# The halo's gated product computed with channels on partitions and its 32 tokens as moving operand, then turned back by four transposes

## The chip, the cores and the metric

The kernel runs on all 8 cores of one Trainium2 chip. Each core works alone on its own 2048 of the 16384 positions, plus a halo of 32 positions ahead of them; nothing is exchanged between cores. The metric is device time in microseconds of the slowest core, over the whole program.

## What is computed

One decoder layer: a mixing sub-layer, a cross-attention into 256 memory tokens, and a SwiGLU feed-forward net, each between two RMS norms with a residual. The change touches the convolution branch (group B) of the mixing:

```python
def parallel_conv_mixer(h, w_mix_in, conv_a_w, conv_b_w, conv_b_b, ln_b_g, ln_b_b, w_mix_out):
    u = jnp.einsum("bsd,dc->bsc", h, w_mix_in)      # 2560 columns
    b_a, c_a, v_a, glu_v, glu_g = jnp.split(u, [D_A, 2 * D_A, 3 * D_A, 3 * D_A + D_B], axis=-1)
    y_a = b_a * causal_dwconv(c_a * v_a, conv_a_w)
    z = glu_v * jax.nn.sigmoid(glu_g)               # 512 channels
    z = causal_dwconv(z, conv_b_w) + conv_b_b       # 31 taps, causal
    y_b = jax.nn.silu(layernorm(z, ln_b_g, ln_b_b))
    y = jnp.concatenate([y_a, y_b], axis=-1)
    return jnp.einsum("bsc,cd->bsd", y, w_mix_out)
```

A convolution with 31 taps needs z of the 30 positions ahead of a core's own ones. Those come from the halo: 32 tokens whose gated product z each core computes for itself, once.

## The kernel before

A core handles its 2048 positions in two tiles of 1024 (`mid(0, ...)`, `mid(1, ...)`), each tile being 8 blocks of 128 tokens. There is no planner: every engine (PE, ACT, DVE, POOL, SP) runs its instructions in the order in which the Python code is written, and waits by semaphores that a small scheduler derives from the buffers' keys. So the order of the calls is the order in each engine's queue.

PSUM is used in two ways. `pair()` hands out three double banks in turn (pp1, pp2, pp3) for matmul results; `tbank()` hands out the two halves of pp0 in turn, for transposes.

The part around the change, in order, for the first tile:

- `glu(7)`: value and gate columns of the last block, 16 matmuls of 512 columns. `glu_ev` evicts: ACT takes tanh of the gate half, DVE multiplies (`stt`) into `zst`. (The gate's sigmoid is made from tanh; the factor 0.5 is in the convolution's weights.)
- `build_wc(0..7)`: eight DVE products of 128x2560 that spread the convolution's taps into `wconv`. Parts 1 and 2 stand behind `glu_ev(7)`, part 3 behind the halo's expansion, parts 4 to 7 in the hooks of `cv_unit`.
- `halo_z` (L552): `hh` holds the 32 halo tokens, transposed. It is the stationary operand (128x32), and `wing`, the weights, moves: 16 matmuls of 512 columns. The result has tokens on 32 partitions and channels in the free dimension. ACT and DVE evict it to `zh` (32x512).
- `halo_expand` (L557): DVE spreads `zh` into `zhe` (32x4096) with a mask, after a small cast to `selT`.
- `mid(0)` (L691): `cv_unit(0, 0)` computes C*v of the first 128 channels: two halves (h = 0, 1) of 16 matmuls, each followed by an ACT copy and a DVE product, then the hook (`build_wc(4 + h)`); then for t = 0 another 16 matmuls of 32 columns with `winc` stationary and `hh` moving, with an ACT copy and a DVE product to `cvh`. Then `halo_zp` (L562): 32 small matmuls that gather `zhe` to the convolution's layout, and a DVE cast into `zp`. Then `z_t` (L571): four groups q of 8 transposes of `zst`, through the two halves of pp0 in turn; q = 0 and 2 are copied out by ACT, q = 1 and 3 by DVE. Then `cv_unit(0, 1)` in the same manner, with `build_wc(6 + h)`, and then the convolution's 160 matmuls (`conv`), which need `zp`, the halo's part of it too.

In the profile matmuls and transposes all bear the lines of the helpers: L374 is `mm`, L433 is `tr`, L354 `act`, L357 `tt`, L367 `stt`, L371 `cp`.

Of the kernel before, what the change touches and what calls it, by code (L numbers as in the profile page):

```python
# [7 lines left out]
BF16 = mybir.dt.bfloat16  # L8
# [5 lines left out]
D = 1024  # L14
# [186 lines left out]
def build_program():  # L201
# [26 lines left out]
    with ExitStack() as stack:  # L228
# [34 lines left out]
        def gbuf(shape, dt, off, keys, group):  # L263
            t = sbt(shape, dt, off)
            nbytes = int(np.prod(shape[1:])) * (4 if dt == F32 else 2)
            for k in keys:
                S.place(k, off, off + nbytes, group)
            return t
# [104 lines left out]
        def mm(out, lhsT, rhs, start, stop, reads, writes, signal):  # L373
            S.op("pe", lambda e: e.matmul(out, lhsT=lhsT, rhs=rhs, start=start, stop=stop), reads, writes, signal)  # L374
# [116 lines left out]
        def evslot():  # L491
            evc[0] += 1
            return evc[0] % 3
# [7 lines left out]
        def glu_mms(lhs, lk, pt, bk, n=128):  # L501
            for h in range(2):
                for kc in range(8):
                    mm(pt[0:n, h * 512:(h + 1) * 512], lhs(kc), wing[:, 2 * h:2 * h + 2, kc, :], kc == 0, kc == 7,
                       [lk, "wg%d" % (4 * h + kc // 4), "wg%d" % (4 * h + 2 + kc // 4)], [bk[h]], kc == 7)

        def glu_evict(pt, bk, groups, nu, n=128):
            s = evslot()
            pv = pt[0:n, 0:nu * 256].rearrange("p (u k c) -> p u k c", k=2, c=128)
            act(ev[0:n, s, 0:nu * 128].rearrange("p (u c) -> p u c", c=128), pv[:, :, 0, :], AF.Tanh,  # L510
                bk[0:(nu + 1) // 2], ["ev%d" % s], scale=0.5)

            def second():
                for u0, u1, out, okey in groups:
                    stt(out.rearrange("p (u g) c -> p u g c", g=8),
                        ev[0:n, s, u0 * 128:u1 * 128].rearrange("p (u g c) -> p u g c", g=8, c=GC), 1.0,
                        pv[:, u0:u1, 1, :].rearrange("p u (g c) -> p u g c", c=GC), ADD, MUL,
                        ["ev%d" % s] + bk[0:(nu + 1) // 2], [okey])
            return second
# [25 lines left out]
        def build_wc(part):  # L545
            gd = NG * ND // 8
            a = part * gd
            tt("dve", wconv[:, a:a + gd, :].rearrange("p a (c r) -> p a c r", r=P),
               wsb[:, a * P:(a + gd) * P].rearrange("p (a r) -> p a r", r=P).unsqueeze(2).broadcast_to([128, gd, GC, P]),
               mkb[:, :, :].unsqueeze(1).broadcast_to([128, gd, GC, P]), MUL, ["mkb", "wsb"], ["wc%d" % part])  # L550

        def halo_z():  # L552
            pt, bk = pair()
            glu_mms(lambda kc: hh[:, kc, :], "hh", pt, bk, HALO)
            return glu_evict(pt, bk, [(0, 4, zh[:, :, :], "zh")], 4, HALO)

        def halo_expand():  # L557
            cp("dve", selT[:, 0:HT], sm[0:HALO, SM_SEL:SM_SEL + HT], ["sm"], ["selT"])
# [3 lines left out]
        def halo_zp():  # L562
            pt, bk = pair()
            for g in range(NG):
                mm(pt[:, g * HT:(g + 1) * HT], zhe[:, g, :, :].rearrange("p s c -> p (s c)"), selT[:, 0:HT], True, True,
                   ["zhe", "selT"], [bk[0]], g == NG - 1)
            cp("dve", zp[:, :, 0:HT], pt[:, 0:NG * HT].rearrange("p (g t) -> p g t", t=HT), [bk[0]], ["zph"])
# [62 lines left out]
        def cv_unit(t, c, after=None):  # L630
            for h in range(2):
                pt, bk = pair()
                hk = ["h%d" % b for b in range(4 * h, 4 * h + 4)]
                for n in range(2):
                    for kc in range(8):
                        mm(pt[:, n * 512:(n + 1) * 512], winc[:, c, kc, n * 128:(n + 1) * 128],
                           hT[:, kc, h * 512:(h + 1) * 512], kc == 0, kc == 7, ["wcv%d" % c] + hk, [bk[n]], kc == 7)
                s = evslot()
                act(ev[:, s, :], pt[:, 0:512], AF.Copy, [bk[0]], ["ev%d" % s])
                tt("dve", cvx[:, c, (2 + 4 * h) * TAU:(6 + 4 * h) * TAU], pt[:, 512:1024], ev[:, s, :], MUL,  # L640
                   ["ev%d" % s, bk[1]], ["cv%d" % c])
                if after is not None:
                    after(h)
            if t == 0:
                pt, bk = pair()
                for n in range(2):
                    for kc in range(8):
                        mm(pt[:, n * 512:n * 512 + HALO], winc[:, c, kc, n * 128:(n + 1) * 128], hh[:, kc, :],
                           kc == 0, kc == 7, ["wcv%d" % c, "hh"], [bk[n]], kc == 7)
                s = evslot()  # L650
                act(ev[:, s, 0:HALO], pt[:, 0:HALO], AF.Copy, [bk[0]], ["ev%d" % s])
                tt("dve", cvh[:, c, :], pt[:, 512:512 + HALO], ev[:, s, 0:HALO], MUL, ["ev%d" % s, bk[1]], ["cvh%d" % c])
                cp("pool", car[:, c, :], cvh[:, c, :].rearrange("p (s t) -> p s t", s=P)[:, 6:8, HT - 1],
                   ["cvh%d" % c], ["car%d" % c])
            v = cvx[:, c, :].rearrange("p (s t) -> p s t", t=TAU)
            cp("pool", v[:, 0:2, 0], car[:, c, :], ["car%d" % c], ["cv%d" % c])
            cp("pool", v[:, 0:2, 1:TAU], v[:, P:P + 2, 0:TAU - 1], ["cv%d" % c], ["cv%d" % c])
            cp("pool", car[:, c, :], v[:, P:P + 2, TAU - 1], ["cv%d" % c], ["car%d" % c])
# [32 lines left out]
        def mid(t, after_conv, fill, fill_t):  # L691
            cv_unit(t, 0, (lambda h: build_wc(4 + h)) if t == 0 else None)
            if t == 0:
                halo_zp()
            z_t(t)
            cv_unit(t, 1, (lambda h: build_wc(6 + h)) if t == 0 else None)
            conv_a(0)
            conv(t)
            fill()
            after_conv()  # L700
            conv_a(1)
            cv_unit(t, 2, lambda h: ln_stats(0, 4) if h == 0 else None)
            ln_rstd(0, 4)
            b_unit(0)
            ln_bias(0, 4)
            ln_stats(4, 8)
            ln_norm(0, 4)
            ln_rstd(4, 8)
            b_unit(1)
            ln_bias(4, 8)  # L710
            conv_a(2)
            fill_t()
            cv_unit(t, 3, lambda h: ln_norm(4, 8) if h == 0 else None)
            conv_a(3)
            b_unit(2)
            n_t(0, 2)
            b_unit(3)
            n_t(2, 4)

        hh = gbuf([128, 8, HALO], BF16, C0 + 4 * D * 4 + 2048, ["hh"], None)  # L720

        def wload_c(c):
            wload("wcv%d" % c, winc[:, c], winc_d[:, c], ["wcv%d" % c])
# [66 lines left out]
        glu_ev(7, *g)  # L790
        build_wc(1)
        build_wc(2)
        halo_z()()
        halo_expand()
        build_wc(3)

        def load_s(s, src, reads=()):
# [463 lines left out]
```

How the kernel before makes its waits and increments, by code:

```python
            def body(e):  # L184
                for (waits, fn, inc) in lists[engname]:
                    for (sk, v) in waits:
                        e.wait_ge(sems[sk], v)
                    if fn is not None:
                        ins = fn(e)
                        if inc is not None:
                            ins.then_inc(sems[inc[0]], inc[1])
```

## Time and profile before

| | us |
|---|---|
| median of 3 runs | 889.1 (887.85 to 889.79) |
| the profiled execution, all cores | 889.61 |
| its spans, core by core | 884.3 to 887.0 |
| core 7, the slowest: span | 887.0 |
| mean granted TensorE clock of the cores | 0.996 to 0.999 |

A span runs from a core's first to its last instruction; the time of an execution also holds what lies around the spans. All rows below are of core 7. In the page's table (core 4, 886.4 us) PE is busy for 849.1 us (96% of the span), DVE for 390.0, ACT for 298.3, POOL for 125.9; the chain that ended last is PE for 92%. The stretch of the change lies between 55 and 85 us, in the fourth and fifth of the 40 slices.

In rows on matmuls, `128*32` is the stationary operand (rows x columns) and `128x512` the moving one. A matmul's duration in a row is from its start to the end of its way through the array; the next one starts long before that end. `LDWEIGHTS` on PEld is the load of the stationary operand, which overlaps PE. "idle" and the name behind "<-" say how long the engine had nothing to do before, and who released it.

### The profile page before, as it was taken

How to read it: one execution, taken by the hardware profiler on the slowest of the kernel's cores; microseconds unless marked ns; L12 is line 12 of the kernel's file. 1: busy time of each engine (PE TensorE's matmuls, PEld its weight loads, DVE VectorE, ACT ScalarE, POOL GpSimd, SP SyncE). 2: the span in 40 equal slices, each digit the busy share in tenths (PEclk: the TensorE clock that was granted, in tenths of full speed). 3: DMA queues.
4: the chain of work that ended last, by engine and by line, in shares of the span. 5: the costliest groups of instructions: out<-in, count | busy, mean ns of one | idle time of the engine just before them, and what ended most of it. 6: DMA issues, size and time to landing. Idle time of an engine off the chain costs nothing.

```text
span 886.4 us, 13126 instructions; the slowest of 8 cores (884.3 to 887.0 us)
## 1 busy us (share of the span) xinstructions
PE 849.1 (96%) x4795; PEld 432.8 (49%) x4872; DVE 390.0 (44%) x500; ACT 298.3 (34%) x544; POOL 125.9 (14%) x290
## 2 busy tenths in 40 slices
PE   2899999999999899999999999999999999999997
PEld 1657444555664455554444444444444444444443
DVE  1477758437547678886522122331232322221122
ACT  2332345532636668765331111221122211111111
POOL 3121113112103132321110010000000000000000
PEclk9999999999999999999999999999999999999999
DMA  9599057368894257877696012122121121210011
GB/s 195 153 179 192 1 185 253 124 128 139 168 221 91 50 148 188 190 153 184 194 182 118 1 72 95 37 60 72 72 95 36 48 84 72 67 53 1 1 48 71
DMA packets 33327, 97.94 MB, mean 110 GB/s; under 512 B 11344, under 2 KB 11472, under 8 KB 32368
## 3 DMA queue, kind: packets, MB, share of 16 engines
q0 software_dynamic: 7344, 33.03, 23.4%
q1 hardware_dynamic: 25920, 64.07, 21.5%
q8 instruction: 39, 0.64, 0.3%
q14 instruction: 24, 0.20, 0.1%
HBM read 107.05 MB, written 20.97 MB: 144 GB/s over the span
## 4 chain that ended last, share of the span: by engine, by line
PE 92%; ACT 3%; issue 2%; DMA 1%; DVE 1%; DVEq 0%; SPq 0%; POOL 0%; POOLq 0%; ACTq 0%
PE pp L374 89%; PE pp L433 3%; ACT t L354 3%; DMA t<-x 1%; DVE t L1003 1%; DVE t L367 0%; ACT L354 0%; DVEq L1193 0%; SPq L377 0%; DVE t L371 0%; POOLq L1193 0%; ACT pp L354 0%; POOL t L357 0%; ACTq L187 0%; POOL t L363 0%
## 5 line engine op out<-in xcount | busy, mean ns | idle before, releaser
L374 PE MATMUL pp<-t,t 128*128 128x512 bf16 (+2 forms) x4195 | 819.2, 354 | 7.9 <-ACT t L354 2.7
L374 PEld LDWEIGHTS pp<-t,t 128*128 128x128 bf16 x4272 | 397.0, 98 | 411.2 <-issue 6.9
L357 DVE TENSOR_TENSOR t<-pp,t 128x512 bf16<-128x512 f32 (+4 forms) x173 | 150.4, 873 | 365.8 <-PE pp L374 194.7
L354 ACT ACTIVATE t<-pp 128x512 f32<-128x512 f32 (+5 forms) x208 | 153.3, 750 | 355.8 <-PE pp L374 336.6
L367 DVE SCALAR_TENSOR_TENSOR t<-t,t,t 128x1024 bf16<-128x1024 f32 (+4 forms) x100 | 126.5, 1271 | 49.3 <-POOL t L357 29.7
L361 POOL TENSOR_SCALAR t<-t 128x1 f32<-128x1 f32 (+2 forms) x102 | 24.7, 242 | 627.5 <-ACT t L354 323.3
L433 PE MATMUL pp<-t,t 128*128 128x128 bf16 (+1 forms) x600 | 43.2, 222 | 23.0 <-DVE t L367 19.8
L354 ACT ACTIVATE pp<-pp 128x1024 f32<-128x1024 f32 (+1 forms) x17 | 16.3, 958 | 142.4 <-PE pp L374 142.4
L357 POOL TENSOR_TENSOR t<-t,t 128x1 f32<-128x1 f32 (+2 forms) x103 | 60.7, 589 | 15.6 <-POOL t L361 0.6
L354 ACT ACTIVATE t<-pp,t 128x256 bf16<-128x256 f32 (+2 forms) x76 | 43.9, 583 | 42.8 <-DVE t L1003 34.2
L354 ACT ACTIVATE t<-t 128x1024 bf16<-128x1024 f32 (+2 forms) x52 | 53.9, 1037 | 8.7 <-DMA t<-x 8.7
L433 PEld LDWEIGHTS pp<-t,t 128*128 128x128 bf16 (+1 forms) x600 | 37.8, 99 | 35.4 <-issue 26.8
L361 DVE TENSOR_SCALAR t<-t,t 128x256 bf16<-128x256 bf16 (+1 forms) x80 | 30.3, 378 | 7.2 <-DVE t L361 0.5
L354 ACT ACTIVATE t<-t,t 128x512 bf16<-128x512 bf16 (+1 forms) x24 | 20.7, 916 | 26.7 <-DVE t L367 16.6
L1003 DVE TENSOR_REDUCE t<-pp 128x4 f32<-128x1024 f32 x16 | 19.5, 1220 | 6.9 <-PE pp L374 6.8
L371 POOL COPY t<-t 128x2 bf16<-128x2 bf16 (+2 forms) x29 | 11.2, 388 | 78.3 <-DVE t L357 72.1
L367 DVE SCALAR_TENSOR_TENSOR t<-t,pp 128x128 bf16<-128x128 f32 (+3 forms) x29 | 12.5, 461 | 22.0 <-ACT t L354 21.4
L371 DVE COPY t<-pp 128x1024 bf16<-128x1024 bf16 x25 | 17.1, 683 | 6.2 <-PE pp L433 6.1
L357 DVE TENSOR_TENSOR t<-t,t 128x2560 bf16<-128x2560 bf16 (+1 forms) x9 | 14.0, 1570 | 0.0
L377 POOL DMA_DIRECT2D t<-w_gu x22 | 13.6, 618 | 0.3 <-issue 0.3
L354 ACT ACTIVATION_READ_ACCUMULATOR t<-pp,t 128x1 f32 x64 | 12.3, 193 | 0.0
L361 DVE TENSOR_SCALAR t<-pp,t 128x1024 bf16<-128x1024 f32 x4 | 5.1, 1284 | 15.1 <-PE pp L374 15.1
(26 smaller groups left out, 65.2 us busy)
## 6 DMA issues: line engine op xcount, KB each, us to landing
t<-x SPq DMA_DIRECT2D x68, 512.0 KB, 6.7
x<-t SPq DMA_DIRECT2D x24, 512.0 KB, 3.6
t<-w_gu POOLq DMA_DIRECT2D x22, 512.0 KB, 6.8
out<-t SPq DMA_DIRECT2D x15, 512.0 KB, 2.8
t<-w_dn POOLq DMA_DIRECT2D x6, 768.0 KB, 20.2
t<-gains SPq DMA_DIRECT2D x6, 512.0 KB, 9.4
t<-w_ing POOLq DMA_DIRECT2D x8, 256.0 KB, 16.5
t<-w_inc POOLq DMA_DIRECT2D x4, 512.0 KB, 10.4
```

Source lines behind the costliest of these rows:

```text
L354: S.op("act", lambda e: e.activation(out=out, in_=in_, func=func, **kw), reads, writes)
L357: S.op(eng, lambda e: e.tensor_tensor(out=out, in0=in0, in1=in1, op=op), reads, writes)
L361: S.op(eng, lambda e: e.tensor_scalar(out=out, in0=in0, scalar1=s1, scalar2=None, op0=op0), reads, writes)
L367: S.op("dve", lambda e: e.scalar_tensor_tensor(out=out, in0=in0, scalar=sc, in1=in1, op0=op0, op1=op1), reads, writes)
L371: S.op(eng, lambda e: e.tensor_copy(out=out, in_=in_), reads, writes)
L374: S.op("pe", lambda e: e.matmul(out, lhsT=lhsT, rhs=rhs, start=start, stop=stop), reads, writes, signal)
L377: return S.dma(eng, sem, lambda e: e.dma_start(out=out, in_=in_), reads, writes)
L433: S.op("pe", lambda e: e.transpose(out, in_, ident[0:n, 0:n]), reads + ["ident"], writes, signal)
L1003: S.op("dve", lambda e: e.tensor_reduce(out=mx[:, m, 0:4], in_=pt[:, :].rearrange("p (h n) -> p h n", h=4), axis=AX.X, op=ALU.max, negate= ...
```

## The change

`halo_z` swaps the operands. For each of 4 chunks of 128 channels, for gate and value (k = 0, 1), and for each of 8 slices of the contraction, the weights of 128x128 are stationary and `hh` moves with its 32 tokens: 64 matmuls of 32 columns in place of 16 of 512. The results lie in 256 columns of one PSUM bank, channels on partitions. ACT's tanh and DVE's product now work on 128x128 elements in place of 32x512 and write `zhT`, a new buffer in a free part of the region that holds `hh`.

A new function `halo_t` turns `zhT` back: four transposes into a half of pp0 (`tbank()`), and a DVE copy of 32x512 from there to `zh`. It stands between `cv_unit(0, 0)` and `z_t(0)`, where `halo_zp` stood. `halo_expand` moves from its place behind `halo_z` to behind `z_t(0)`, and `halo_zp` into the hook of `cv_unit(0, 1)` behind its first half, ahead of `build_wc(6)`.

```diff
--- before.py
+++ after.py
@@ -551,8 +551,23 @@
 
         def halo_z():
             pt, bk = pair()
-            glu_mms(lambda kc: hh[:, kc, :], "hh", pt, bk, HALO)
-            return glu_evict(pt, bk, [(0, 4, zh[:, :, :], "zh")], 4, HALO)
+            for c in range(4):
+                for k in range(2):
+                    for kc in range(8):
+                        mm(pt[:, (2 * c + k) * HALO:(2 * c + k + 1) * HALO], wing[:, c, kc, k * 128:(k + 1) * 128],
+                           hh[:, kc, :], kc == 0, kc == 7, ["hh", "wg%d" % (2 * c + kc // 4)], [bk[0]],
+                           c == 3 and k == 1 and kc == 7)
+            s = evslot()
+            pv = pt[:, 0:8 * HALO].rearrange("p (c k n) -> p c k n", k=2, n=HALO)
+            tv = ev[:, s, 0:4 * HALO].rearrange("p (c n) -> p c n", n=HALO)
+            act(tv, pv[:, :, 0, :], AF.Tanh, [bk[0]], ["ev%d" % s], scale=0.5)
+            stt(zhT[:, :, :], tv, 1.0, pv[:, :, 1, :], ADD, MUL, ["ev%d" % s, bk[0]], ["zhT"])
+
+        def halo_t():
+            pv, bk = tbank()
+            for c in range(4):
+                tr(pv[0:HALO, c * 128:(c + 1) * 128], zhT[:, c, :], 128, ["zhT"], [bk], c == 3)
+            cp("dve", zh[:, :, :].rearrange("p g c -> p (g c)"), pv[0:HALO, 0:512], [bk], ["zh"])
 
         def halo_expand():
             cp("dve", selT[:, 0:HT], sm[0:HALO, SM_SEL:SM_SEL + HT], ["sm"], ["selT"])
@@ -691,9 +706,17 @@
         def mid(t, after_conv, fill, fill_t):
             cv_unit(t, 0, (lambda h: build_wc(4 + h)) if t == 0 else None)
             if t == 0:
-                halo_zp()
+                halo_t()
             z_t(t)
-            cv_unit(t, 1, (lambda h: build_wc(6 + h)) if t == 0 else None)
+            if t == 0:
+                halo_expand()
+
+            def hook(h):
+                if h == 0:
+                    halo_zp()
+                build_wc(6 + h)
+
+            cv_unit(t, 1, hook if t == 0 else None)
             conv_a(0)
             conv(t)
             fill()
@@ -718,6 +741,8 @@
             n_t(2, 4)
 
         hh = gbuf([128, 8, HALO], BF16, C0 + 4 * D * 4 + 2048, ["hh"], None)
+
+        zhT = gbuf([128, 4, HALO], BF16, C0 + 4 * D * 4 + 2560, ["zhT"], None)
 
         def wload_c(c):
             wload("wcv%d" % c, winc[:, c], winc_d[:, c], ["wcv%d" % c])
@@ -790,8 +815,7 @@
         glu_ev(7, *g)
         build_wc(1)
         build_wc(2)
-        halo_z()()
-        halo_expand()
+        halo_z()
         build_wc(3)
 
         def load_s(s, src, reads=()):
```

On PE, from the halo tokens' own transposes to the last products of `cv_unit(0, 1)` (t1_43 is `wing`, t39_81 the transposed tokens `hT`, t72_114 `hh`, t2_44 `winc`, t26_68 `selT`, t12_54 `zst`, t73_115 `zhT`, t69_111 the unit matrix; the order of before with - and of now with +):

```order
 L374 MATMUL pp3<-t1_43,t39_81 128x512 x16
-L374 MATMUL pp1<-t1_43,t72_114 32x512 x16
+L374 MATMUL pp1<-t72_114,t1_43 128x32 x64
 L374 MATMUL pp2<-t39_81,t2_44 128x512 x16
 L374 MATMUL pp3<-t39_81,t2_44 128x512 x16
 L374 MATMUL pp1<-t72_114,t2_44 128x32 x16
-L374 MATMUL pp2<-t26_68,t21_63 128x4 x32
+L433 MATMUL pp0<-t69_111,t73_115 32x128 x4
 L433 MATMUL pp0<-t69_111,t12_54 128x128 x32
-L374 MATMUL pp3<-t39_81,t2_44 128x512 x16
+L374 MATMUL pp2<-t39_81,t2_44 128x512 x16
+L374 MATMUL pp3<-t26_68,t21_63 128x4 x32
```

The halo's matmuls become 64 short ones at the same place, four transposes through pp0 come ahead of the 32 of `z_t`, and the 32 gathering matmuls (128x4) move from ahead of `z_t` to behind the first 16 of `cv_unit(0, 1)`.

On DVE, from the product of `glu(7)` (t12_54) to the cast into `zp` (t14_56), before (t4_46 is `wconv`, t22_64 `zh`, t21_63 `zhe`, t41_83 the C*v products, t24_66 `cvh`, t14_56 `zp`, t26_68 `selT`):

```order
L367 SCALAR_TENSOR_TENSOR t12_54<-t50_92,pp3 128x32x16
L357 TENSOR_TENSOR t4_46<-t42_84,t43_85 128x2560 x2
L367 SCALAR_TENSOR_TENSOR t22_64<-t50_92,pp1 32x512
L371 CAST t26_68<-t65_107 32x4
L357 TENSOR_TENSOR t21_63<-t22_64,t44_86 32x4096
L357 TENSOR_TENSOR t4_46<-t42_84,t43_85 128x2560
L357 TENSOR_TENSOR t41_83<-pp2,t50_92 128x512
L357 TENSOR_TENSOR t4_46<-t42_84,t43_85 128x2560
L357 TENSOR_TENSOR t41_83<-pp3,t50_92 128x512
L357 TENSOR_TENSOR t4_46<-t42_84,t43_85 128x2560
L357 TENSOR_TENSOR t24_66<-pp1,t50_92 128x32
L371 CAST t14_56<-pp2 128x32x4
```

and now, from the two `wconv` products behind that product of `glu(7)` to the expansion (t73_115 is `zhT`):

```order
L357 TENSOR_TENSOR t4_46<-t42_84,t43_85 128x2560 x2
L367 SCALAR_TENSOR_TENSOR t73_115<-t50_92,pp1 128x128
L357 TENSOR_TENSOR t4_46<-t42_84,t43_85 128x2560
L357 TENSOR_TENSOR t41_83<-pp2,t50_92 128x512
L357 TENSOR_TENSOR t4_46<-t42_84,t43_85 128x2560
L357 TENSOR_TENSOR t41_83<-pp3,t50_92 128x512
L357 TENSOR_TENSOR t4_46<-t42_84,t43_85 128x2560
L357 TENSOR_TENSOR t24_66<-pp1,t50_92 128x32
L371 COPY t22_64<-pp0 32x512
L371 COPY t14_56<-pp0 128x8x128 x2
L371 CAST t26_68<-t65_107 32x4
L357 TENSOR_TENSOR t21_63<-t22_64,t44_86 32x4096
```

The copy of 32x512 into t22_64 is new; it stands behind the fifth `wconv` product of this list and the `cvh` product, and ahead of the copies of `z_t`. The expansion of 32x4096 moves from ahead of the third `wconv` product to behind the copies of `z_t`.

## Rows read from the trace of the kernel before

**Rows 1.** Stretches of core 7: PE busy (instructions), granted clock, DMA share, GB/s.
```profile
20.00:30.00 10.00, 7.58 (x41) 1.00 0.98 259
...
55.00:95.00 40.00, 39.18 (x386) 1.00 0.82 171
```

**Rows 2.** Chain that ended last, core 7, 51 to 92 us: start us, us, what.
```profile
51.65 3.45 PE pp L374 x16
...
55.39 15.40 PE pp L374 x112
70.80 0.57 PE pp L433 x8
...
71.45 1.03 ACT t L354
72.48 0.14 issue
```

**Rows 3.** PE timeline, core 7: start, us, instruction, xcount [idle before <-releaser].
```profile
70.73 1.07 PE L433 MATMUL pp<-t,t 128*128 128x128 bf16 x16
72.61 1.05 PE L433 MATMUL pp<-t,t 128*128 128x128 bf16 x16 [0.82 <-ACT t L354]
73.50 10.71 PE L374 MATMUL pp<-t,t 128*128 128x512 bf16 x106
...
25.88 1.01 PE L433 MATMUL pp<-t,t 128*128 128x128 bf16 x8 [2.42 <-DVE t L367]
```

**Rows 4.** PE and PEld groups by form, 55 to 95 us: xcount | busy, mean ns | idle.
```profile
L374 PE MATMUL pp<-t,t 128*128 128x128 bf16 x160 | 9.1, 219 | 0.0
...
L374 PE MATMUL pp<-t,t 128*128 128x32 bf16 x32 | 1.1, 176 | 0.0
L374 PE MATMUL pp<-t,t 32*128 32x4 bf16 x32 | 0.9, 159 | 0.0
...
L374 PEld LDWEIGHTS pp<-t,t 128*128 128x128 bf16 x298 | 20.0, 98 | 12.5 <-issue 0.4
```

**Rows 5.** The same view in 5 ns of the first 16-matmul burst, 69.700 to 69.705 us.
```profile
L374 PE MATMUL pp<-t,t 128*128 128x32 bf16 x7 | 0.3, 176 | 0.0
```

**Rows 6.** DVE timeline, core 7, columns as in rows 3.
```profile
63.30 0.68 DVE L367 SCALAR_TENSOR_TENSOR t<-t,pp 32x512 bf16<-32x512 f32 x1
63.90 0.15 DVE L371 CAST t<-t 32x4 bf16<-32x4 f32 x1
64.08 3.68 DVE L357 TENSOR_TENSOR t<-t,t 32x4096 bf16<-32x4096 bf16 x2
...
69.70 0.69 DVE L357 TENSOR_TENSOR t<-pp,t 128x512 bf16<-128x512 f32 x1
70.31 1.48 DVE L357 TENSOR_TENSOR t<-t,t 128x2560 bf16<-128x2560 bf16 x1
71.71 0.18 DVE L357 TENSOR_TENSOR t<-pp,t 128x32 bf16<-128x32 f32 x1
71.81 0.28 DVE L371 CAST t<-pp 128x128 bf16<-128x128 f32 x1
...
73.77 0.69 DVE L371 COPY t<-pp 128x1024 bf16<-128x1024 bf16 x1 [1.09 <-PE pp L433]
77.23 0.69 DVE L357 TENSOR_TENSOR t<-pp,t 128x512 bf16<-128x512 f32 x1 [2.76 <-PE pp L374]
```

**Rows 7.** DVE groups by form, 20 to 180 us: xcount | busy, mean ns | idle.
```profile
L357 DVE TENSOR_TENSOR t<-pp,t 128x1024 f32<-128x1024 f32 x8 | 9.8, 1222 | 6.5 <-ACT t L354 6.5
...
L357 DVE TENSOR_TENSOR t<-pp,t 128x512 bf16<-128x512 f32 x8 | 5.5, 686 | 4.7 <-PE pp L374 4.2 <-ACT t L354 0.5
L371 DVE COPY t<-pp 128x1024 bf16<-128x1024 bf16 x5 | 3.4, 687 | 3.6 <-PE pp L433 3.6
L367 DVE SCALAR_TENSOR_TENSOR t<-t,pp 128x128 bf16<-128x128 f32 x12 | 2.8, 282 | 10.4 <-ACT t L354 10.4
...
L357 DVE TENSOR_TENSOR t<-t,t 32x4096 bf16<-32x4096 bf16 x1 | 2.3, 2279 | 0.0
```

## The prediction

> **What bounds the kernel now.** I read the stretches first. Between 55 and 95 us, which holds everything that the change touches, PE is busy for 39.18 of 40.00 us at a granted clock of 1.00 [rows 1]: the full one of TensorE's two levels, 2.4 GHz. The chain that ended last [rows 2] says the same in order of time: PE alone from 55.39 us for 15.40 us, then eight transposes, then ACT's copy of the first group of `z_t` (1.03 us), then PE again. So whatever shortens PE's work here counts, as long as PE does not then wait for somebody. The only wait in the stretch is 0.82 us in the middle of `z_t` [rows 3]: the third group of transposes needs the half of pp0 from which ACT is still copying the first. Then I read DVE's timeline [rows 6], since the change puts one more DVE instruction between two steps of PE. From 63.30 us on DVE goes from one instruction to the next without idle time until the copies of `z_t`. Its queue is full of `wconv` products of 1.4 us each that nobody needs yet, and whatever stands behind them has to wait.
>
> **The halo's matmuls.** Before: 16 matmuls of 512 columns. Sixteen such take 3.45 us (216 ns each) [rows 2]. Now: 64 of 32 columns, each with its own 128x128 weights. The trace has that very form, in the bursts of 16 that `cv_unit` runs for the halo. Its duration is 176 ns and 7 are under way at any instant [rows 5], so one starts every 25 ns. Two such bursts keep PE busy for 1.1 us, or 34 ns each with the way through the array counted twice; the 32 matmuls of 4 columns take 0.9 us, or 28 ns each [rows 4]. I take 27 ns: 64 x 27 = 1.73 us, so 1.72 us less on PE. The ends are 25 (1.60 us) and 34 (2.18 us); the trace has bursts of 16 directly followed by 32, not of 64, so a higher end stands among the rivals.
>
> The Trainium skill ("TensorE: Matmul & The Clock Gate", section "Wait — 56ns, not 53.3ns?") gives a floor of about 25 ns from start to start of small matmuls, which the trace bears out with 25; it also says that with hardware decode off the sequencer spends about 62 ns on each matmul. By that the halo would take 64 x 62 = 3.97 us, 2.24 more than my term, and the kernel 891.4; the 28 ns of the gathering matmuls here speak against it.
>
> **The eviction.** ACT's tanh and DVE's product shrink: 676 ns or so of DVE (0.68, [rows 6]) against 282 ns for a 128x128 product [rows 7]. Nobody waits for either. The product stands behind `wconv` products until 63.2 us, and `zhT` is wanted only some 5 us later. This part is worth nothing in itself.
>
> **The transposes back.** Four transposes with 128 moving columns. The convolution's 160 of that width take 9.1 us [rows 4], so 57 ns each: 0.23 us more on PE. I allow nothing else for them, since `zhT` is long there.
>
> **The new copy, and who stands behind it.** `halo_t` takes one half of pp0. The first group of `z_t` gets the other, and the second group gets the half of `halo_t` again, so it has to wait until DVE has copied `zh` out of it. That copy stands in DVE's queue behind the C*v product of the second half of `cv_unit(0, 0)`, the `wconv` product from its hook and the small `cvh` product. I follow it in the clock of core 7:
>
> - Before, `z_t` starts at 70.73 [rows 3]. Going back by the gathering matmuls (0.90) and by 16 of 32 columns (0.45), the second half of `cv_unit(0, 0)` ended at 69.38. Now it ends 1.72 earlier, at 67.66.
> - PE: 16 small matmuls to 68.11, four transposes to 68.34, first group of `z_t` (8 x 56 ns) to 68.79. Then it waits.
> - DVE: a product starts 0.28 us after PE's last matmul (73.50 + 16 x 0.216 = 76.95 against 77.23, [rows 3, 6]), so at 67.94. From it to the `wconv` product 0.61, from there to `cvh` 1.40, to the next 0.10 [rows 6]: the copy starts at 70.05.
> - The copy: 1222 ns for 1024 and 686 for 512 elements of a product give 150 ns fixed; a copy of 1024 bf16 takes 687 [rows 7], so 0.52 ns an element, and 512 take 0.42 us. Bounds are 0.28 (the 128-element cast) and 0.69. It ends at 70.47, and a PE that waited starts 0.14 later [rows 2]: 70.61. **PE waits 1.82 us.**
> - Second and third group to 71.50; ACT has copied the first by about 70.1, so the old wait of 0.82 goes. The fourth needs the half of the second: DVE's copy starts 0.27 after that group (73.50 against 73.77, [rows 3, 6]), at 71.32, takes 0.69, and with 0.14 PE goes on at 72.15. A new wait of 0.65. `z_t` ends at 72.60.
>
> Before, it ended at 73.50 [rows 3]: 0.90 earlier now. But the gathering matmuls, 0.90 us, no longer lie in front of it; they come behind the next 16 matmuls. Sum so far: 0.00.
>
> **The moved expansion.** It was hidden and far ahead; now it has to be ready when the first half of `cv_unit(0, 1)` ends at 72.60 + 3.45 = 76.05. DVE: last copy of `z_t` at 72.87, next at 73.48, cast 0.18 (63.90 to 64.08), expansion 2.28 [rows 6, 7]: it ends at 75.94, with 0.14 at 76.08. A tie, with 0.03 us of waiting. The cover is PE's 16 matmuls, and there is nothing to spare: each tenth that DVE comes later is paid. The gathering then takes the 0.90 already counted. Behind it stand the cast into `zp`, `wconv` parts 6 and 7, and the product of the second half. PE's second half gives DVE 3.45 us for 0.28 + 1.4 of work, so the queue is caught up, and the convolution finds the engines as before. POOL and SP get nothing new.
>
> **The sum.** Halo matmuls -1.72, transposes back +0.23. Waits in `z_t`, all from start to start: +1.82 + 0.65 for the new ones, and for the old one 72.61 less 71.63 (70.73 + 16 x 56 ns), 0.98; the 0.82 of its row counts from the end of the last transpose's way through the array. Together +1.49. Wait for the expansion +0.03. The sum is +0.03 us. The profiled execution took 889.61 us and would take 889.6; that is 0.5 above the median of the runs, 889.1, so I forecast **889.1**. By the bounds: 25 ns gives -0.13, 34 ns +0.45, the copy at 0.28 or 0.69 gives -0.14 or +0.27.
>
> **Rivals.**
>
> *The gain comes through.* If DVE served the copy at once (say the `wconv` product were not between, which the order excludes), PE would wait only for ACT as before: -1.72 + 0.23 = -1.5 us, with 25 ns -1.6. That gives 887.5 to 887.6. Against it speaks DVE's queue, which is in order in every row; for it only that PE's early start might let DVE's queue slip differently than I draw it.
>
> *Short matmuls do not keep their pace.* In a burst of 64 the instructions or the weights' loads may not come fast enough. The loads take 98 ns each when alone [rows 4] and overlap only because many are under way; a pair of load and matmul of 128 columns takes 57 ns. At 57 ns the halo takes 3.65 us, 1.92 above my 1.73. PE then still waits the same 1.8 us, because DVE's copy is released by PE, and the kernel ends at 891.1 (with the 0.03 of the sum); wholly exposed, at 98 ns, 6.27 in place of 1.73, 893.7. It decides from 55 ns on, where the loss is 28 ns x 64 = 1.8 us.  Against it: 48 short matmuls in a row already run at 25 to 28 ns while the DMA engines are just as busy.
>
> *The expansion comes late.* If DVE is later by half a microsecond (a copy that waits longer, a slower product beside DMA traffic), PE waits for `zhe` behind 16 matmuls: +0.5, 889.6. Likely enough, but too small to be told from nothing.
>
> *The clock falls* in the new wait of 1.8 us. PE idled 2.42 us at 25.9 us, and the granted clock there and around it reads 1.00 [rows 1, 3]. I give it no chance of its own.
>
> **How the numbers follow.** A measurement here tells about 0.2% (1.8 us) from no change; the largest gain that the rows allow, 1.6 us, is under that. Chances: the wait eats the gain, with or without a late expansion, 0.84 (all of it within 0.2%); the gain comes through 0.07 (887.5: at the edge, and half of it would read as same); short matmuls slow 0.07 (mostly over 0.2%); something small elsewhere 0.02. The three runs shown spread from 887.85 to 889.79, so about 0.03 on each side goes to readings that stray past 0.2%. Together: faster 0.07, same 0.84, slower 0.09. The range goes from the gain that comes through (887.5) to slow matmuls at 57 ns (891.1), which leaves out 1 to 2 in 10.
>
> **What would show it.** In the profile of the changed kernel: a group of 64 matmuls 128x32, some 1.7 us long, ahead of `cv_unit(0, 0)`; ACT's and DVE's halo instructions at 128x128; in `z_t` of the first tile a PE idle of about 1.8 us released by DVE's copy (L371) after the first eight transposes, one of 0.65 by DVE's copy before the last eight, and none by ACT; the first 512-column matmuls of `cv_unit(0, 1)` some 0.9 us earlier than at 73.50 on a core with the same start; little or no idle before the 128x4 matmuls. I am wrong if the idle in `z_t` is much shorter (then it is faster), if the 64 take over 3 us, or if PE waits for `zhe` by a microsecond or more.

## The result, and the profile of the changed kernel

| | before | changed |
|---|---|---|
| median of 20 runs, us | 888.45 | 890.54 |
| ratio to before on the same chip | | 1.0014 (1.0008 to 1.0021) |
| profiled execution, us | 889.61 | 889.46 |
| its spans, core by core, us | 884.3 to 887.0 | 883.4 to 887.9 |
| mean granted clock of its cores | 0.996 to 0.999 | 0.993 to 0.999 |

By the ratio, which sets runs against runs of before on the same chip and is the measure here (the medians lie 2.1 us apart), the changed kernel is slower by 0.14%, about 1.2 us, where no change at all was forecast. One run of the kernel before (1004.9 us) and two of the changed one (about 1060 us), in which one die ran at a lower clock, are left out of the ratio. The 0.14% are less than the 0.2% that I called the limit of what can be told, but 19 runs against 18 tell it: the interval does not reach 1. So something costs a microsecond or more that is not in my sum.

Around the change nearly everything is as forecast. The chain of the slowest core, core 5 (start us, us, what), now goes from PE to DVE and back, twice, where in [rows 2] it went once over ACT:

```profile
53.53 12.46 PE pp L374 x128
...
66.38 1.58 DVE t L357 x2
67.97 0.33 DVE t L371
68.30 0.14 issue
...
69.14 0.70 DVE t L371
...
69.98 0.76 PE pp L433 x8
```

PE's timeline of the same core shows the two waits, both released by DVE's copies (L371), 1.56 and 0.50 us of idle in place of the 0.82 for ACT in [rows 3]:

```profile
65.92 0.95 PE L433 MATMUL pp<-t,t 128*32 128x128 bf16 x12
68.43 1.05 PE L433 MATMUL pp<-t,t 128*128 128x128 bf16 x16 [1.56 <-DVE t L371]
69.98 0.76 PE L433 MATMUL pp<-t,t 128*128 128x128 bf16 x8 [0.50 <-DVE t L371]
70.53 5.62 PE L374 MATMUL pp<-t,t 128*128 128x512 bf16 x30
```

DVE's timeline is the queue that I drew, to a few hundredths (compare [rows 6]): the product of the second half of `cv_unit(0, 0)`, `wconv` part 5, the `cvh` product, then the copy of `zh` in 0.40 us (0.42 in the forecast).

```profile
65.78 0.69 DVE L357 TENSOR_TENSOR t<-pp,t 128x512 bf16<-128x512 f32 x1 [0.80 <-PE pp L374]
66.38 1.48 DVE L357 TENSOR_TENSOR t<-t,t 128x2560 bf16<-128x2560 bf16 x1
67.78 0.18 DVE L357 TENSOR_TENSOR t<-pp,t 128x32 bf16<-128x32 f32 x1
67.88 0.40 DVE L371 COPY t<-pp 32x512 bf16<-32x512 bf16 x1
69.14 0.69 DVE L371 COPY t<-pp 128x1024 bf16<-128x1024 bf16 x1 [0.86 <-PE pp L433]
...
71.52 2.27 DVE L357 TENSOR_TENSOR t<-t,t 32x4096 bf16<-32x4096 bf16 x1
75.83 0.69 DVE L357 TENSOR_TENSOR t<-pp,t 128x512 bf16<-128x512 f32 x1 [2.04 <-PE pp L374]
```

The expansion (71.52 us) is done at 73.79. And the groups by form, 55 to 95 us: 96 matmuls of 32 columns (64 of the halo, 32 of `cv_unit`) and four transposes of `zhT`:

```profile
L374 PE MATMUL pp<-t,t 128*128 128x32 bf16 x96 | 2.9, 176 | 0.0
...
L433 PE MATMUL pp<-t,t 128*32 128x128 bf16 x4 | 0.4, 222 | 0.0
```

Two rows above do not fit the sum, though. The last eight transposes take 0.55 us to the start of the next matmuls (69.98 to 70.53) where eight take 0.45. And DVE's product of the first half of `cv_unit(0, 1)` starts at 75.83, while 16 matmuls from 70.53 with DVE's 0.28 would end at 74.27: it comes 1.56 us late. The stretches of core 5 say why (PE busy with its instructions, granted clock, DMA share, GB/s):

```profile
66.00:70.00 4.00, 1.94 (x29) 1.00 1.02 210
70.00:71.00 1.00, 1.00 (x10) 0.65 0.99 213
71.00:73.00 2.00, 2.00 (x6) 0.50 1.09 223
73.00:74.00 1.00, 1.00 (x4) 0.65 1.08 205
74.00:80.00 6.00, 6.00 (x56) 1.00 1.03 212
```

The granted clock falls to 0.50, the lower of the two levels (1.2 GHz), in the 71st microsecond, and is back at full in the 74th. At half speed 0.70 us in the first of these rows, 2.0 in the second and 0.70 in the third cost 0.35 + 1.0 + 0.35 = 1.7 us. Six of the eight cores show this. Core 1 does not:

```profile
70.00:71.00 1.00, 0.50 (x10) 1.00 1.09 195
71.00:73.00 2.00, 2.00 (x16) 1.00 1.10 222
```

```profile
69.38 1.05 PE L433 MATMUL pp<-t,t 128*128 128x128 bf16 x16 [1.56 <-DVE t L371]
70.93 0.61 PE L433 MATMUL pp<-t,t 128*128 128x128 bf16 x8 [0.50 <-DVE t L371]
71.37 4.82 PE L374 MATMUL pp<-t,t 128*128 128x512 bf16 x49
```

It has the same two waits and the same order, and its last eight transposes take 0.44 us to the next matmuls.

For the whole stretch I take two marks on PE that both kernels have: the start of the eight transposes of the halo tokens (32x32), ahead of `glu(7)`, and the start of the first transposes of `n_t`, behind the convolution and most of the tile's work. Before, on core 7, 59.69 us lie between them (all eight cores: 59.68 or 59.69):

```profile
55.03 0.36 PE L433 MATMUL pp<-t,t 32*128 32x32 bf16 x8
...
114.72 1.06 PE L433 MATMUL pp<-t,t 128*128 128x128 bf16 x16
```

Changed kernel, core 1, without the fall of the clock, 59.53:

```profile
54.12 0.36 PE L433 MATMUL pp<-t,t 32*128 32x32 bf16 x8
...
113.65 1.06 PE L433 MATMUL pp<-t,t 128*128 128x128 bf16 x16
```

Changed kernel, core 5, with it, 61.14:

```profile
53.17 0.36 PE L433 MATMUL pp<-t,t 32*128 32x32 bf16 x8
...
114.31 1.06 PE L433 MATMUL pp<-t,t 128*128 128x128 bf16 x16
```

So the change as such is worth -0.16 to -0.23 us here (cores 1 and 2), and each of the six cores whose clock falls ends up 1.3 to 1.5 us behind the kernel before; the fall itself costs 1.5 to 1.7 us.

The kernel before has such a fall too, at another place, and in both kernels alike. PE waits 2.42 us at about 25 us there, on every core. Its core 5, timeline and stretch:

```profile
24.82 0.61 PE L433 MATMUL pp<-t,t 128*128 128x128 bf16 x8 [2.42 <-DVE t L367]
```

```profile
25.00:30.00 5.00, 5.00 (x37) 0.66 0.93 242
```

Cores 0 to 3, 5 and 6 show this; cores 4 and 7 are dealt with below, where the prediction is answered. 0.34 of 5.00 us are 1.7 us lost, the price of one fall.

### The profile page after: what moved, and what is told of

The parts are those of the page before. It is cut to its first block, busy times and chain, and to the rows that moved or that the text cites. A ratio compares the mean times of both kernels' runs of the same rounds, so it can differ in the third digit from the quotient of the medians.

```text
span 887.9 us, 13309 instructions; the slowest of 8 cores (883.4 to 887.9 us)
## 1 busy us (share of the span) xinstructions
PE 854.0 (96%) x4924; PEld 433.5 (49%) x4924; DVE 390.0 (44%) x501; ACT 298.1 (34%) x544; POOL 125.1 (14%) x290
## 4 chain that ended last, share of the span: by engine, by line
PE 92%; ACT 3%; DVE 1%; DMA 1%; issue 1%; DVEq 0%; SPq 0%; POOL 0%; POOLq 0%; ACTq 0%
PE pp L374 89%; PE pp L433 3%; ACT t L354 3%; DMA t<-x 1%; DVE t L1027 1%; DVE t L367 0%; DVE t L357 0%; DVE t L371 0%; ACT L354 0%; DVEq L1217 0%; SPq L377 0%; POOLq L1217 0%; ACT pp L354 0%; POOL t L357 0%; ACTq L187 0%
## 5 line engine op out<-in xcount | busy, mean ns | idle before, releaser
L374 PE MATMUL pp<-t,t 128*128 128x512 bf16 (+3 forms) x4320 | 825.5, 352 | 3.8 <-ACT t L354 2.7
L354 ACT ACTIVATE t<-t,t 128x512 bf16<-128x512 bf16 (+1 forms) x24 | 20.7, 916 | 25.6 <-DVE t L367 16.6
L371 POOL COPY t<-t 128x2 bf16<-128x2 bf16 (+2 forms) x29 | 11.0, 380 | 79.8 <-DVE t L357 73.6
L367 DVE SCALAR_TENSOR_TENSOR t<-t,pp 128x128 bf16<-128x128 f32 (+2 forms) x29 | 12.1, 448 | 21.3 <-ACT t L354 20.8
L371 DVE COPY t<-pp 128x1024 bf16<-128x1024 bf16 (+1 forms) x26 | 17.5, 672 | 6.6 <-PE pp L433 6.4
## 6 DMA issues: line engine op xcount, KB each, us to landing
t<-w_ing POOLq DMA_DIRECT2D x8, 256.0 KB, 17.3
```

The costliest lines, as they stand in the source:

```text
L354: S.op("act", lambda e: e.activation(out=out, in_=in_, func=func, **kw), reads, writes)
L367: S.op("dve", lambda e: e.scalar_tensor_tensor(out=out, in0=in0, scalar=sc, in1=in1, op0=op0, op1=op1), reads, writes)
L371: S.op(eng, lambda e: e.tensor_copy(out=out, in_=in_), reads, writes)
```

## The experiments

**First theory, the clock.** The added idle time of PE in `z_t` lets the granted clock fall on most cores; without the fall the change would be neutral. **Rival:** the 64 + 16 short matmuls ahead of `z_t` let it fall, whether PE then waits or not. (A third reading, that the waits themselves cost the microsecond, already has core 1 against it.) All counts of falls below are of the profiled execution's eight cores, and "stretch" is the one between the two marks.

### The idle time filled

```diff
@@ z_t, t == 0, behind the transposes of q == 0
+fp, fb = pair()
+rrp[0] -= 1
+for i in range(8):
+    mm(fp[:, 0:512], winc[:, 0, i, 0:128], hT[:, i, 0:512], i == 0, i == 7, ..., [fb[0]], i == 7)
```

> The changed kernel with 8 matmuls of 512 columns (1.73 us, result thrown away) on PE between the first and the second group of z_t, where PE waits for DVE's copy. Theory, the clock: the changed kernel is slower only because PE's idle time in z_t lets the granted clock fall to 0.5 in 6 of 8 cores; here PE is busy, the clock stays at 1.00 on all cores, the stretch from the halo tokens' transposes to the first transposes of n_t takes about 59.5 us on every core (59.5 without and 61.1 with the fall in the changed kernel) and the time is that of the kernel before, ratio 0.999 to 1.000. Rival, the short matmuls: the 64 + 16 short matmuls before z_t are what lets the clock fall; then it falls as before, 61.1 us in most cores, ratio 1.001 to 1.002.

Ratio 0.9995 (0.9986 to 1.0004). No core's clock falls in `z_t`; the stretch is 59.46 us on every core. On core 1, PE's timeline and two rows of its stretches:

```profile
68.31 0.95 PE L433 MATMUL pp<-t,t 128*32 128x128 bf16 x12
69.10 1.89 PE L374 MATMUL pp<-t,t 128*128 128x512 bf16 x8
70.83 1.06 PE L433 MATMUL pp<-t,t 128*128 128x128 bf16 x16
```

```profile
70.00:71.00 1.00, 1.00 (x9) 1.00 0.98 231
71.00:73.00 2.00, 1.50 (x25) 1.00 1.07 271
```

The second group of transposes (70.83) starts 2.52 us after the transposes back (68.31); in the changed kernel it was 2.51 (65.92 to 68.43 on core 5). DVE's copy comes no sooner, PE does 1.7 us of useless work in the meantime, and the kernel is as fast as before. The waiting as such is not what costs the time, and the 80 short matmuls alone do not let the clock fall.

### The copy no longer held up

`wconv` part 5 is wanted only by the third quarter of the convolution. Here it goes behind the expansion:

```diff
-cv_unit(t, 0, (lambda h: build_wc(4 + h)) if t == 0 else None)
+cv_unit(t, 0, (lambda h: build_wc(4) if h == 0 else None) if t == 0 else None)
...
             if t == 0:
                 halo_expand()
+                build_wc(5)
```

> The changed kernel with wconv part 5 moved on DVE from the hook of cv_unit(0, 0) to behind the halo's expansion, so that DVE's copy of zh is not held up by it. Theory, the clock: PE's wait before the second group shrinks from 1.8 us (start to start) to about 0.4, with some wait for ACT left before the third, the clock does not fall on any core, the stretch takes about 58.1 us (59.69 before), ratio 0.998 to 0.999. Rival, the short matmuls: clock falls in most cores, stretch 59.7, ratio 1.000.

Ratio 0.9988 (0.9978 to 0.9998). No fall in `z_t`, stretch 58.05 to 58.13 us, 1.6 under that of the kernel before. PE's timeline, core 4:

```profile
68.51 0.61 PE L433 MATMUL pp<-t,t 128*128 128x128 bf16 x8 [0.16 <-DVE t L371]
69.61 1.05 PE L433 MATMUL pp<-t,t 128*128 128x128 bf16 x16 [0.50 <-ACT t L354]
70.72 9.47 PE L374 MATMUL pp<-t,t 128*128 128x512 bf16 x100
```

The idle time of 1.56 us is down to 0.16, and 0.50 for ACT stand where 0.82 were.

### The wait alone, in the kernel before

```diff
 halo_zp()
+pv, bk = tbank()
+for c in range(4):
+    tr(pv[0:HALO, c * 128:(c + 1) * 128], hh[:, c, :], 128, ["hh"], [bk], c == 3)
+cp("dve", zh[:, :, :].rearrange("p g c -> p (g c)"), pv[0:HALO, 0:512], [bk], ["zh"])
 z_t(t)
```

> The kernel before with only the changed kernel's four transposes and DVE copy added ahead of z_t (of hh, result unused); halo matmuls, gathering and expansion as before. PE should wait about 1.1 us for DVE's copy before the second group and 0.6 before the last, z_t ends 1.1 us later than before: stretch 60.8 us without a fall of the clock (59.69 before). Theory, the clock by idle time: it falls on some cores, fewer than 6 since the idle is shorter, 1.6 us each, 62.4 there. Rival, the short matmuls: no falls, 60.8 on every core.

One run, 890.25 us (the kernel before on the same chip had a median of 888.65). Stretch 60.72 to 60.73 us on six cores, as forecast to 0.1; the clock fell on two, 61.83 and 61.75 (62.4 was forecast for such cores). There the fall came earlier, so that the last transposes ran slowly and the wait for DVE in front of the last group went, which is why the loss is 1.1 and not 1.6. PE's timeline of core 1, where 24 transposes follow the first wait in one piece:

```profile
71.45 2.96 PE L433 MATMUL pp<-t,t 128*128 128x128 bf16 x24 [0.88 <-DVE t L371]
```

So the wait brings the fall without the halo's 64 short matmuls. It does not need the new operands.

### The transposes back in a bank of their own

```diff
 def halo_t():
-    pv, bk = tbank()
+    hp_, hb = pair()
+    pv, bk = hp_[:, 0:512].bitcast(BF16), hb[0]
```

and the call moves from ahead of `z_t(0)` to behind its second group.

> The changed kernel with the four transposes back moved behind the second group of z_t and into a PSUM bank of their own (pair()), so that no group of z_t waits for the copy of zh. Theory, the clock: PE's idle in z_t is that of the kernel before, at most 0.8 us for ACT, partly filled by the four transposes, no core falls, cv_unit(0, 1) starts some 1.3 us earlier than in the changed kernel, stretch about 58.2 us, ratio 0.998 to 0.999. Rival, the short matmuls: clock falls in most cores, 59.8 us.

Ratio 0.9977 (0.9967 to 0.9987): faster than before by 0.23%, 2 us. Stretch 58.18 us on all cores, no fall in `z_t`. PE's timeline, core 2; the 20 transposes are the first two groups and the four back:

```profile
67.83 1.38 PE L433 MATMUL pp<-t,t 128*128 128x128 bf16 x20
69.70 0.61 PE L433 MATMUL pp<-t,t 128*128 128x128 bf16 x8 [0.49 <-ACT t L354]
70.70 0.61 PE L433 MATMUL pp<-t,t 128*128 128x128 bf16 x8 [0.39 <-DVE t L371]
```

The median went by 2.0 us where the stretch went by 1.5. The rest is within the interval.

### How long the idle time is

Two more kernels change only the length of the wait before the second group. Twice the DVE work ahead of the copy:

```diff
-cv_unit(t, 0, (lambda h: build_wc(4 + h)) if t == 0 else None)
+cv_unit(t, 0, (lambda h: build_wc(4) if h == 0 else (build_wc(5), build_wc(6))) if t == 0 else None)
```

(part 6 leaves its old hook), and half of part 5 ahead, the other half behind the expansion.

> The changed kernel with wconv part 6 too ahead of the copy of zh on DVE (in the hook of cv_unit(0, 0), behind part 5). PE's idle before the second group grows from 1.56 to about 2.97 us. Theory, the clock by idle time: it falls on all or nearly all 8 cores (6 of 8 in the changed kernel's profile); stretch 60.9 us without and 62.5 with the fall. Rival, the fall does not depend on the length of the idle: still on 5 or 6 of 8 cores.

> The changed kernel with only half of wconv part 5 ahead of the copy of zh, the other half behind the expansion. PE's idle before the second group shrinks from 1.56 to about 0.86 us, the 0.50 before the last stays. Theory, the clock by idle time: it falls on fewer cores than in the changed kernel, 0 to 2 of 8; stretch 58.8 us without and 60.4 with the fall. Rival, the length does not matter: 5 or 6 of 8.

The longer wait: ratio 1.0024 (1.0010 to 1.0038), idle 2.96 us, the clock fell on 8 of 8 cores, stretch 61.8 to 63.2 us (62.5 expected). The shorter: ratio 0.9984 (0.9971 to 0.9998), idle 0.89 and 0.50 us, 0 of 8, stretch 58.78 to 58.79. PE's timelines, core 6 of the first and core 7 of the second:

```profile
70.68 1.40 PE L433 MATMUL pp<-t,t 128*128 128x128 bf16 x16 [2.96 <-DVE t L371]
72.23 1.01 PE L433 MATMUL pp<-t,t 128*128 128x128 bf16 x8 [0.15 <-DVE t L371]
```

```profile
68.99 1.05 PE L433 MATMUL pp<-t,t 128*128 128x128 bf16 x16 [0.90 <-DVE t L371]
```

More DVE work ahead of the copy (+1.4 us) and more falls; less work and none. (How much the second half of this is worth is said under the next heading.)

### The old operands under the same wait

Here the halo is computed as before (16 matmuls of 512 columns), and all the rest is as in the changed kernel, with the four transposes (now of `hh`) and their copy. The copy goes to a corner of `zhe`, which the expansion overwrites; that part of the edit is not in the cut below.

```diff
 def halo_z():
     pt, bk = pair()
-    for c in range(4):
-        ...
-    stt(zhT[:, :, :], tv, 1.0, pv[:, :, 1, :], ADD, MUL, ["ev%d" % s, bk[0]], ["zhT"])
+    glu_mms(lambda kc: hh[:, kc, :], "hh", pt, bk, HALO)
+    glu_evict(pt, bk, [(0, 4, zh[:, :, :], "zh")], 4, HALO)()
```

> The changed kernel with the halo's operands as in the kernel before (16 matmuls of 512 columns, evicted straight to zh), while the four transposes (of hh, result unused), their copy on DVE and the moved gathering and expansion stay. The waits in z_t should stay at 1.56 and 0.50 us, with 64 short matmuls fewer ahead of them and 1.75 us more of PE work. Theory, the clock by idle time alone: falls on about as many cores as in the changed kernel, 4 to 8 of 8; stretch 61.3 us without and 62.9 with the fall. Rival, the 64 short matmuls are part of the cause: no or hardly any core falls, 61.3.

Ratio 1.0011 (0.9998 to 1.0024); the clock fell on 3 of 8, against 6 of 8 in the changed kernel with the same idle time. Stretch 61.5 without and up to 63.2 with the fall. Three against six is little to go by, so both kernels were profiled twice more:

> The changed kernel once more, to count on how many cores the clock falls in z_t (6 of 8 in its first profile). If the short matmuls ahead of the idle time are part of the cause, 5 to 7 of 8 here and in the next, against 2 to 4 with the old operands; if idle time alone decides and 6 against 3 was chance, both give about 4 or 5 of 8. The stretch: 59.5 us without, 61.1 with the fall.

> The version with the old operands (16 matmuls of 512 columns for the halo, same waits in z_t) once more. Short matmuls part of the cause: 2 to 4 of 8 cores fall; idle time alone: about as many as in the changed kernel, 4 or 5. Stretch 61.5 us without, 63.2 with the fall.

> A third profile of the changed kernel, for the same count: 5 to 7 of 8 if the short matmuls are part of the cause, 4 or 5 if not.

> A third profile of the version with the old operands: 2 to 4 of 8 if the short matmuls are part of the cause, 4 or 5 if not.

Changed kernel 2 and 6 of 8, old operands 0 and 0. PE's timeline of core 7 of the second profile with the old operands shows the same two waits:

```profile
71.11 1.05 PE L433 MATMUL pp<-t,t 128*128 128x128 bf16 x16 [1.56 <-DVE t L371]
72.66 0.61 PE L433 MATMUL pp<-t,t 128*128 128x128 bf16 x8 [0.50 <-DVE t L371]
```

Together 14 of 24 against 3 of 24. (Changed kernel, second profile: 2 of 8, under the 5 to 7 expected of the reading that the short matmuls count. Old operands, second and third: none, under the 2 to 4 of that reading and the 4 or 5 of the other.) The bare counts speak for the short matmuls. The traces' records of the granted clock give another reason for the difference.

**Each core has fixed moments at which its clock can change.** On any one core the changes between 1.00 and 0.50 lie whole numbers of one and the same step apart, to 0.003 us, in all 14 profiles (112 cores), whatever the program does between them. In the first profile of the changed kernel, core 0 falls at 25.27 and at 69.64 us and core 7 at 26.01 and at 70.38: 44.37 us apart on both, although the second fall comes 16.62 us behind the first mark on core 0 and 17.24 on core 7. So for a core that did not fall one can tell from its other changes when it could have. Counted from the first mark:

| kernel | moments of the cores that fell, us | nearest moments of the cores that did not, us |
|---|---|---|
| changed, 3 profiles | 16.62 to 17.24 (14 cores) | 16.54, and from 17.32 (10 cores) |
| idle filled | none fell | 16.70, 17.10, 17.16, 17.28 |
| old operands, 3 profiles | 17.38, 19.24, 19.35 | up to 17.34, and from 19.54 |
| before with a wait | 17.38, 17.54 | up to 17.14, and from 19.24 |
| half of part 5 late | none fell | 16.53, 16.59 |
| parts 5 and 6 ahead | 15.83, 16.31, 16.34, and 16.82 to 17.50 (8 cores) | none |

In the changed kernel one number per core separates the 14 that fell from the 10 that did not, without an exception: whether such a moment lies between about 16.6 and 17.3 us. There the second wait of `z_t` ends (at 16.81; the first ends at 15.26). With the old operands both waits end 2.06 us later, so that stretch would lie from about 18.7 to 19.4 us. Only two of the 24 cores had a moment in it, 19.24 and 19.35, and both fell. The third, at 17.38, fell at the end of the first wait, a place at which no core of the changed kernel had a moment. None of the 112 cores has one between 17.54 and 19.24 us. So 3 of 24 in place of 14 of 24 follows from where the waits lie against these moments, and the two counts are no sign that the short matmuls matter; whether they have a part at all, no run here shows.

The same reading makes one experiment stronger and one weaker. With the idle time filled, three cores had their moment at 16.70, 17.10 and 17.16, where all 14 cores of the changed kernel fell, and none of the three did: PE's work is what kept the clock up. With half of part 5 late everything in `z_t` lies 0.67 us earlier, and of its eight cores one had a moment well in the stretch that corresponds (16.53, between 15.9 and 16.6), and a second (16.59) at its edge. Its "0 of 8" is the word of one or two cores and does not show that a wait of 0.89 us is too short. In the kernels with part 5 late and with the bank of their own `z_t` is earlier too, and the same doubt stands. With parts 5 and 6 ahead, cores fell whose moments lie at 15.83, 16.31 and 16.34, while six cores of the changed kernel had theirs at 15.83 to 16.38 and did not fall: a longer wait is hit by more of the moments.

### Both measures together

The version with its own bank, and `wconv` part 5 behind the expansion:

> The version with the four transposes in a bank of their own behind the second group of z_t, and wconv part 5 moved behind the expansion as well. The 0.39 us that PE waited there for DVE's copy of the second group should go, ACT's 0.50 stay: stretch 57.8 to 57.9 us (58.18 and 58.06 for either measure alone), no core with a fall in z_t, ratio 0.997 to 0.998. Rival: the wconv part is then in the way behind the expansion and PE waits elsewhere; stretch 58.2 or more.

Ratio 0.9977 (0.9964 to 0.9989), stretch 57.63 us on all eight cores (57.8 to 57.9 expected), no fall in `z_t`. One wait is left, ACT's, of 0.49 us.

It beats the kernel before by as much as the bank alone; the half microsecond more in the stretch cannot be told in the total. It ran on another chip, where the kernel before took 892.26 us.

### All of it in one table

Short matmuls are those of 32 or 4 columns between `cv_unit(0, 0)` and the first group of `z_t`, with the halo's 64 where they stand ahead of `cv_unit(0, 0)`.

| kernel | short matmuls | PE idle in `z_t`, us | clock falls, cores | stretch without / with, us |
|---|---|---|---|---|
| before | 16 + 32 | 0.82 | 0 of 8 | 59.69 |
| changed | 64, 16 | 1.56 + 0.50 | 14 of 24 | 59.5 / 61.1 |
| idle filled | 64, 16 | 0.50 | 0 of 8 | 59.46 |
| part 5 late | 64, 16 | 0.16 + 0.50 | 0 of 8 | 58.1 |
| half of part 5 late | 64, 16 | 0.89 + 0.50 | 0 of 8 | 58.8 |
| parts 5 and 6 ahead | 64, 16 | 2.96, up to 0.4 more | 8 of 8 | 61.8 to 63.2 with |
| old operands, same waits | 16 | 1.56 + 0.50 | 3 of 24 | 61.5 / 62.6 to 63.2 |
| before with a wait | 16 + 32 | 0.88 + 0.50 | 2 of 8 | 60.7 / 61.8 |
| own bank | 64, 16 | 0.49 + 0.39 | 0 of 8 | 58.18 |
| own bank, part 5 late | 64, 16 | 0.49 | 0 of 8 | 57.63 |

## Why the prediction was wrong, point by point

**The halo's matmuls: the right direction, the saving forecast a sixth too small.** From the first of the 64 to the next matmul behind them are 1.60 us in the changed kernel (cores 1 and 5), 25 ns each, where 27 were taken: the lower of the stated ends. The 16 of 512 columns took 3.65 us between their neighbours in the kernel before (core 7), not 3.45, as 0.1 us is lost at either end of them. So the new form saves 2.05 us, not 1.72. The rival with slow short matmuls is out. The Trainium skill ("TensorE: Matmul & The Clock Gate", section "Wait — 56ns, not 53.3ns?") has a floor of about 25 ns from start to start, and these rows agree; its 62 ns, which it ties to hardware decode being off, are not seen here (no run shows how that setting stood).

**The transposes back:** 0.33 us from the first of the four to the next group, 0.23 forecast.

**The wait for the copy: right in mechanism, place and size.** Forecast from start to start 1.82 and 0.65 us; measured in the same way 1.73 and 0.65 (core 1; the rows' 1.56 and 0.50 count from the end of the last transpose's way through the array). The old wait for ACT went, as said.

**The moved expansion: right.** No idle time of PE ahead of the 128x4 matmuls. DVE was ready some 0.2 us before PE on core 1, and 1.6 us before it on core 5, whose clock had fallen.

**The sum without the clock: right.** +0.03 us forecast, -0.16 to -0.23 measured in the stretch.

**The clock: wrong, and this is the step that failed.** The prediction names it as a rival, puts its cost at nothing and says "I give it no chance of its own", from one reading: 2.42 us of idle at 25.9 us on core 7 with the granted clock at 1.00 [rows 1, 3]. That reading is wrong. The trace of core 7 holds no record of the granted clock ahead of 31.32 us, and the view prints 1.00 where there is none. What PE did shows the level. The row of [rows 3] itself has the eight transposes behind that wait at 1.01 us, 107 ns from start to start; later on the same core, with the clock on record at 1.00, eight take 0.61 us, 56 ns from start to start:

```profile
32.44 0.61 PE L433 MATMUL pp<-t,t 128*128 128x128 bf16 x8
```

So core 7 was at the lower level through that wait and had nothing to lose. Core 4 is in the same case (first record at 30.74 us). On the six other cores of the same profile the clock did fall, within 1.2 us of the end of the same wait of 2.42 us, as core 5 shows above. The profile of before held the answer: in it a wait of PE of 2.42 us is followed by a fall on all six cores that had a clock to lose, at a price of 1.7 us. In the changed kernel the waits of 1.56 and 0.50 us, with short PE work between them, brought it on 14 of 24 cores at 1.5 to 1.7 us each. From those rows the forecast would have been 0 to +1.7 us, around 890, with a good chance for a fall.

**Why 1.6 us on some cores move the slowest.** The time is that of the slowest of eight cores. In the 18 timed executions of the changed kernel that the ratio uses, 73 of 144 cores have a mean clock of 0.995 or less, which in its three profiles is the mark of a core that fell in `z_t`, and in all 18 the slowest core is one of them. In 25 executions of the kernel before beside the first experiments there is no such core among 200, and none among the 80 of the version with its idle time filled. Cores start apart by two or three microseconds (the first mark lies between 52.0 and 54.4 us in the changed kernel's profile), so a fall on an early core is hidden, and one on a late core is paid in full. That is how about half the cores with 1.4 us more come to some 1.2 us in the total.

**The chances.** 0.84 for "within 0.2%" holds in the letter, since 1.0014 lies in it, but it was given to the wrong mechanism, and the sign was there to be told.

## What to carry to other kernels

A change that shortens PE's work and lengthens a wait behind it is not neutral where the two sum to zero: the longer PE idles, the more cores lose their clock, and a fall in `z_t` costs 1.0 to 1.7 us per core here. Look for what stands in the queue of the engine that ends the wait. In this kernel one DVE product of 1.4 us that nobody needed yet turned a gain of 0.1 to 0.2% into a loss, and moving it, or giving the transposes a bank of their own, turned it back. And where eight cores run, read the clock on all of them, not on the slowest alone, and hold it against the time from start to start of matmuls of one form: 107 ns or 56 ns for a transpose of 128 columns tells the level even where the trace has no record of the clock.

## What the runs showed of the hardware that I had not expected

- **Which cores fall is settled by when each core's clock can change, not by the program alone.** With instructions and waits equal to 0.01 us, some cores keep 1.00 and others fall to 0.50; the table of moments above separates the two without an exception in the changed kernel. So a count such as 6 of 8, or 0 of 8, depends on where a wait lies as well as on how long it is. What moves these moments against the program from one execution to the next, no run here shows. The Trainium skill ("TensorE: Matmul & The Clock Gate", section "What's actually happening") says that activity opens the clock's gate and its lack closes it, with these two levels; these runs agree with it.
- **A second place.** At 289 us both kernels have PE idle times of about a microsecond, for other reasons. In the changed kernel's first profile cores 5 and 7 have another fall there. Core 5, then core 1, in the same stretch:

```profile
289.00:293.00 4.00, 4.00 (x13) 0.60 0.00 0
```

```profile
289.00:293.00 4.00, 4.00 (x21) 1.00 0.00 0
```

  The mean clock of 0.60 over 4 us costs 1.6 us. It is found on 7 of 24 cores of the changed kernel, 0 of 8 of the kernel before, and on 4 of 8 of the kernel before with a wait added. Nothing was changed there. The moments account for it as well. PE waits 0.85 and then 0.99 us there. Counted from the end of the first of these waits, the 21 cores of all 14 profiles that fall have their moment at 2.05 to 2.49 us, just behind the second, and of the other 91 none has one between 2.03 and 2.57. An edit at 70 us that shifts the rest of the program by a microsecond or so changes which cores those are. What part of the 1.2 us this second place has, stays open.
- **A clock between the two levels.** The chip of the second set of experiments granted one die 0.81 for stretches of 3.5 to 7 us, in each of its four profiles. Its times are higher (892.26 us for the kernel before), which fits, and only their ratios are used here.
